# The down projection of a decoder layer as three direct pieces and two Strassen stages, with the sums of activation quarters on GpSimd

## The chip, the cores and the metric

One Trainium2 chip, one core. The kernel is a program of five engines written out by hand: TensorE (PE, matmuls; PEld its weight loads), VectorE (DVE), ScalarE (ACT), GpSimd (POOL) and SyncE (SP), which here only issues DMAs. The metric is the device time of one execution in microseconds (us).

## The reference

One layer of a decoder in float32: a token mixer, a cross attention and a gated channel mixer, each on a normalised input and added to the residual stream, then a last normalisation. The change concerns the last product, `w_down`, of shape 5632 x 2048, on 512 tokens:

```python
D_MODEL, SEQ, D_FF = 2048, 512, 5632

def swiglu(h, w_gate_up, w_down):
    gu = h @ w_gate_up
    g, u = gu[..., :D_FF], gu[..., D_FF:]
    return (jax.nn.silu(g) * u) @ w_down

def reference(x, mem, g_mix, w_in, ...):
    ...
    h = h + swiglu(rms_norm(h, g_ffn[l]), w_gate_up[l], w_down[l])
    return rms_norm(h, g_final)
```

## The kernel before

**Precision.** Every float32 operand is split into a high part `hi` (ACT copies it into the float32r type) and a remainder `lo` (DVE subtracts, `lo = x - hi`). A product is the three matmuls hi*hi, hi*lo and lo*hi, summed in PSUM.

**Direct form** (`columns`, L695 to L709). A weight tile of 128 rows by 512 columns, one *step*, is cut into four column tiles j. For each j three matmuls run over 512 tokens (L702, L703, L704): 12 matmuls a step, into the four PSUM banks of a group. DVE and ACT split the weights one step at a time into a ring of four slots (`w_hi`, `w_lo`; `SPL = 4`), so they can be at most four steps ahead of PE. Weights come in by SP, two steps in a DMA of 512 KB, into `raw`, which holds four such pairs.

**Strassen stage** (`Stage`, `product`, `products`). Where the contraction runs over 16 tiles of 128 and the result has two column tiles ("gate" and "up") and two token halves of 256, a block needs seven products of half size instead of eight: P1, Q5, P2, P6, P7, P4, P3 in this order in PE, interleaved with those of the next block (`cycle_products`). A product is eight *wide* matmuls (L936: hi weights by 512 columns, which are the hi and the lo part of 256 tokens side by side) and eight *narrow* ones (L947: lo weights by 256 columns). P6, P7 and P4 start with the narrow ones. Three of the seven (P1, P2, P4) use quarters of the activations as they are, the other four use sums s1 to s4 of quarters. For each block DVE splits 14 half products of weights (`block_lo`, L1945), forms four sums of weights (`sum_x1` to `sum_x4`, L1953 to L1972) and takes the results out of PSUM (`gate_first`, `gate_joined`, `up_first`, `up_second`, `up_joined`), with ACT's copies of partial sums and `gate_second` beside them. The weight slots are eight. The mixer's gates (`mix`, 16 blocks) and gate and up of the channel mixer (`ffn`, 40 blocks) have this form.

**Down projection.** The 44 tiles of the hidden activation have been spilled to DRAM (`hidden_spilled`, by POOL, one when `hidden_out` has made it) and come back by `hidden_load`; ACT and DVE split them again (`hidden_hi` L1548, `hidden_lo` L2296). It is in the direct form: two halves hh of 22 tiles (`HH = 22`), in each four column groups c, in each 22 steps k, 176 steps in all. DVE adds each finished group to the residual `acc`, which has been reloaded from DRAM (`down_out`, `last_sum` L2447).

**The end.** The last sums, their squares (ACT) and the addition of squares (DVE `add_square`, L2160) lead to one small set of matmuls (`square_sums`), 16 transposes, the scaling and the stores.

**Order.** Every engine runs its list in order and waits on semaphores. SP's queue holds all loads in one order, POOL's queue the spills. A wait in ACT's or DVE's list holds back everything that stands behind it, the splitting of weights for PE above all.

Of the kernel before, what the change touches and what calls it, by code (L numbers as in the profile page):

```python
# [22 lines left out]
F32 = mybir.dt.float32  # L23
# [25 lines left out]
HH = HT // 2  # L49
# [37 lines left out]
G_LAST = G_DOWN + 4  # L87
# [34 lines left out]
class Stage:  # L122
# [5 lines left out]
    last_group: int  # L128
    reg_a: list
# [43 lines left out]
def build(nc, x, mem, g_mix, w_in, conv_w, sinks, w_attn_o, w_conv_o, w_out, g_xattn, g_mem,  # L173
          w_xq, w_xkv, w_xo, g_ffn, w_gate_up, w_down, g_final, rope, out):
    with ExitStack() as ctx:
# [57 lines left out]
        up_t = at("up_t", 120 * KB, [P, 2, 2, SEQ])  # L233
        gfin = at("gfin", 176 * KB, [P, D])
# [65 lines left out]
        PLACES = [s_res[:, i, :, :] for i in range(12)] + [h_both[:, :, k, :] for k in range(0, KT, 2)]  # L300
        PLACES += [h_both[:, :, k, :] for k in range(1, KT, 2)] + [s_res[:, i, :, :] for i in (14, 15)]

        def place(h):

            return h if h < len(PLACES) else h - len(PLACES)
# [27 lines left out]
        def regions(X, Y):  # L333
# [5 lines left out]
        s_x = [sem(f"x_loaded{t}") for t in range(TT)]  # L339
# [79 lines left out]
        mix = Stage(0, KT, 4, mix_snap, G_OPROJ + 7, *regions(A, B), m_both,  # L419
                    *mix_slots, *block_sems)  # L420
        ffn = Stage(KT, BLOCKS, 0, ffn_snap, G_U0, *regions(B, A), s_both,
                    *ffn_slots, *block_sems)
        s_xsum = sem("x_summed")
# [20 lines left out]
        s_hld = [sem(f"hidden_loaded{i}") for i in range(8)]  # L444
# [11 lines left out]
        def _(sp):  # L456
# [118 lines left out]
            def hidden_load(h):  # L575

                n = place(h)
                if h >= len(PLACES):
                    sp.wait_ge(s_used, B_DOWN + 3 * HH + n + 1 - (G_DOWN + 3))
                elif h < 4:  # L580
                    sp.wait_ge(ffn.used, ffn.number("Q5", BLOCKS - 1) + 2)
                elif h < 8:
                    sp.wait_ge(ffn.used, ffn.number("P6", BLOCKS - 1) + 2)
                elif h < 12:
                    sp.wait_ge(ffn.used, ffn.number("P7", BLOCKS - 1) + 2)
                else:
                    sp.wait_ge(ffn.used, ffn.halves())
                sp.wait_ge(s_hsp[h % 2], 16 * (h // 2 + 1))
                if h >= 8:
                    sp.wait_ge(s_hld[h % 8], 16 * (h // 8))  # L590
                sp.dma_start(PLACES[n][:, 1, :].bitcast(F32), hid_dram[h]).then_inc(s_hld[h % 8], 16)

            def down_load(hh, c, p):

                load((B_DOWN + HH * (4 * hh + c)) // 2, 0, None, p, wd, hh * HH * P + 256 * p, 512 * c)

            for p in range(RAW):
                sp.wait_ge(ffn.lo, ffn.number("P7" if p == 1 else "P3" if p == 3 else "P4", BLOCKS - 2) + 2)
                sp.dma_start(raw[:, p, :, :], wd[256 * p:256 * p + 256, 0:512].rearrange("(b p) n -> p b n", p=P)).then_inc(s_raw[p], 16)
            for h in range(12):  # L600
                hidden_load(h)
            for hh in range(2):
                for c in range(4):
                    for p in range(HH // 2):
                        if hh == 0 and c == 0 and 4 <= p < 9:
                            hidden_load(2 * p + 4)
                            hidden_load(2 * p + 5)
                        if hh or c or p >= RAW:
                            down_load(hh, c, p)
                        if hh == 0 and 1 <= c < 3 and p < 4:  # L610
                            hidden_load(HH + 4 * (c - 1) + p)
                        if hh == 0 and p == 9:
                            if c == 0:
                                for i in range(2):
                                    sp.wait_ge(s_hsp[i], 16 * (HT // 2))
                            sp.dma_start(acc[:, 4 * c:4 * c + 4, :], acc_dram[c]).then_inc(s_ald[c], 16)
                        if hh and c == 0 and 2 * p + len(PLACES) < HT:
                            hidden_load(len(PLACES) + 2 * p)
                            hidden_load(len(PLACES) + 2 * p + 1)
# [8 lines left out]
        def _(pool):  # L628
# [55 lines left out]
            pool.wait_ge(ffn.used, ffn.halves())  # L684
# [4 lines left out]
        def _(pe):  # L689
# [185 lines left out]
            def product(st, name, b):  # L875

                first, last = 4 * (st.last_group - 1), 4 * st.last_group
                if name == "P1":
                    r = st.reg_a[b % 2]
                    if b == 0:  # L880
                        pe.wait_ge(s_freed, first + 1)
                        if st is mix:
                            pe.wait_ge(s_ulo, KT)
                    elif b == 1:
                        pe.wait_ge(s_freed, first + 4)
                    else:
                        pe.wait_ge(st.g2, st.base + b - 1)
                elif name == "Q5":
                    r = st.reg_c[b % 2]
                    if b == 0:  # L890
                        pe.wait_ge(s_freed, first + 2)
                        if st is mix:
                            pe.wait_ge(s_mslo, 8)
                        else:
                            pe.wait_ge(s_slo, 16)
# [28 lines left out]
                if st is ffn and b == 0 and name == "P2":  # L924
                    pe.wait_ge(s_pl, KT)
                n, on = st.number(name, b), name in ("P6", "P7", "P4", "P3")
# [158 lines left out]
            for hh in range(2):  # L1085
                for c in range(4):
                    g = G_DOWN + 4 * hh + c
                    b0 = B_DOWN + HH * (4 * hh + c)
# [1410 lines left out]
```

## Time and profile before

| | |
|---|---|
| time, median of 3 runs | 2650.07 us (2649.94 to 2652.64) |
| the profiled execution, first to last instruction | 2649.0 us |
| PE busy | 2625.9 us (99%), 13393 matmuls |
| DVE busy | 1858.1 us (70%) |
| ACT busy | 1222.7 us (46%) |
| POOL busy | 56.0 us (2%) |
| DMA | 343.18 MB, mean 130 GB/s |

The profiled execution's own time is its span, 2649.0 us, 1.1 us below the median of the runs; the profile shows nothing around the span. Shares of busy time are averages over stages with different limits: in the two Strassen stages DVE is busy nearly all the time, in the down projection about a third of it. Matmuls overlap in the pipeline, so the duration of one (0.39 us) is longer than its distance from the next; the pace is read from start to start.

### The profile page before, as it was taken

How to read it: one execution, taken by the hardware profiler on the slowest of the kernel's cores; microseconds unless marked ns; L12 is line 12 of the kernel's file. 1: busy time of each engine (PE TensorE's matmuls, PEld its weight loads, DVE VectorE, ACT ScalarE, POOL GpSimd, SP SyncE). 2: the span in 40 equal slices, each digit the busy share in tenths (PEclk: the TensorE clock that was granted, in tenths of full speed). 3: DMA queues.
4: the chain of work that ended last, by engine and by line, in shares of the span. 5: the costliest groups of instructions: out<-in, count | busy, mean ns of one | idle time of the engine just before them, and what ended most of it. 6: DMA issues, size and time to landing. Idle time of an engine off the chain costs nothing.

```text
span 2649.0 us, 35447 instructions
## 1 busy us (share of the span) xinstructions
PE 2625.9 (99%) x13393; PEld 2243.3 (85%) x13393; DVE 1858.1 (70%) x3163; ACT 1222.7 (46%) x2275; POOL 56.0 (2%) x106
## 2 busy tenths in 40 slices
PE   8999999999999999999999999999999999999998
PEld 7888788888888888888888888888888888888887
DVE  5557876755999964457889999999999973234334
ACT  6335553434555543345655555555555542233221
POOL 0000000000000000000000000000000000000000
PEclk9999999999999999999999999999999999999999
DMA  6332222545445473233444343443434463343222
GB/s 232 95 95 81 72 80 83 194 145 164 143 140 166 132 276 110 96 105 121 149 116 135 116 134 110 122 129 116 133 111 121 131 222 135 124 143 120 96 99 92
DMA packets 331933, 343.18 MB, mean 130 GB/s; under 512 B 11420, under 2 KB 240884, under 8 KB 329204
## 3 DMA queue, kind: packets, MB, share of 16 engines
q1 hardware_dynamic: 320756, 292.68, 35.4%
q0 software_dynamic: 11008, 48.24, 4.7%
q8 instruction: 107, 1.75, 0.3%
q14 instruction: 62, 0.51, 0.1%
HBM read 304.17 MB, written 36.70 MB: 129 GB/s over the span
## 4 chain that ended last, share of the span: by engine, by line
PE 98%; DVE 1%; ACT 0%; issue 0%; DMA 0%; DVEq 0%; ACTq 0%
PE bank L936 27%; PE bank L702 16%; PE bank L703 16%; PE bank L704 16%; PE bank L947 14%; PE bank L717 2%; PE bank L719 2%; PE bank L718 2%; PE bank L823 0%; PE bank L756 0%; DVE y_out L2474 0%; PE bank L1051 0%; PE bank L1023 0%; PE bank L811 0%; PE bank L837 0%
## 5 line engine op out<-in xcount | busy, mean ns | idle before, releaser
L1666 DVE TENSOR_TENSOR w_lo<-raw,w_hi 128x512 fp32r<-128x512 f32 x352 | 243.7, 692 | 478.3 <-ACT w_hi L1130 477.5
L1130 ACT ACTIVATE w_hi<-raw 128x512 fp32r<-128x512 f32 x352 | 222.3, 631 | 584.7 <-PE bank L704 580.1
L702 PE MATMUL bank<-h_both,w_hi 128*128 128x512 f32 x864 | 340.9, 395 | 0.3 <-DVE v_c L1828 0.3
L703 PE MATMUL bank<-h_both,w_hi 128*128 128x512 f32 x864 | 336.9, 390 | 0.0
L704 PE MATMUL bank<-h_both,w_lo 128*128 128x512 f32 x864 | 336.6, 390 | 0.0
L1945 DVE TENSOR_TENSOR w_lo<-braw,w_hi 128x512 fp32r<-128x512 f32 x392 | 251.3, 684 | 9.5 <-ACT w_hi L1308 9.5
L1668 DVE SCALAR_TENSOR_TENSOR w_lo<-raw,par,w_hi 128x512 fp32r<-128x512 f32 x208 | 155.2, 750 | 144.0 <-ACT w_hi L1130 142.9
L1130 ACT ACTIVATE w_hi<-raw,par 128x512 fp32r<-128x512 f32 x208 | 149.3, 721 | 194.9 <-PE bank L704 123.3
L1308 ACT ACTIVATE w_hi<-braw 128x512 fp32r<-128x512 f32 x392 | 222.3, 625 | 34.2 <-PE bank L947 16.1
L704 PEld LDWEIGHTS bank<-h_both,w_lo 128*128 128x128 f32 x864 | 162.2, 188 | 34.9
L702 PEld LDWEIGHTS bank<-h_both,w_hi 128*128 128x128 f32 x864 | 162.3, 188 | 32.5 <-issue 0.5
L703 PEld LDWEIGHTS bank<-h_both,w_hi 128*128 128x128 f32 x864 | 162.4, 188 | 31.1
L1945 DVE TENSOR_TENSOR h_both<-braw,h_both 128x512 fp32r<-128x512 f32 x280 | 179.3, 684 | 0.0
L1308 ACT ACTIVATE h_both<-braw 128x512 fp32r<-128x512 f32 x280 | 158.7, 625 | 14.9 <-PE bank L947 12.4
L702 PE MATMUL bank<-s_res,w_hi 128*128 128x512 f32 x416 | 161.8, 389 | 0.0
L703 PE MATMUL bank<-s_res,w_hi 128*128 128x512 f32 x416 | 161.8, 389 | 0.0
L704 PE MATMUL bank<-s_res,w_lo 128*128 128x512 f32 x416 | 161.8, 389 | 0.0
L936 PE MATMUL bank<-s_both,w_hi 128*128 128x512 f32 x640 | 157.6, 391 | 0.0
L936 PE MATMUL bank<-s_both,h_both 128*128 128x512 f32 x640 | 157.5, 391 | 0.0
L1329 ACT ACTIVATE snap_b<-bank 128x512 f32<-128x512 f32 x54 | 32.3, 599 | 260.6 <-PE bank L936 260.6
L936 PEld LDWEIGHTS bank<-s_both,h_both 128*128 128x128 f32 x640 | 117.6, 188 | 22.7
L936 PEld LDWEIGHTS bank<-s_both,w_hi 128*128 128x128 f32 x640 | 117.6, 188 | 22.7
(289 smaller groups left out, 5343.9 us busy)
## 6 DMA issues: line engine op xcount, KB each, us to landing
braw<-in_w_gate_up_dram SPq DMA_DIRECT2D x160, 512.0 KB, 5.2
raw<-in_w_down_dram SPq DMA_DIRECT2D x88, 512.0 KB, 3.6
raw<-in_w_in_dram SPq DMA_DIRECT2D x80, 512.0 KB, 3.5
braw<-in_w_in_dram SPq DMA_DIRECT2D x64, 512.0 KB, 5.0
raw<-in_w_out_dram SPq DMA_DIRECT2D x32, 512.0 KB, 3.6
hidden_spilled<-up_t POOLq DMA_DIRECT2D x44, 256.0 KB, 5.7
raw<-in_w_attn_o_dram SPq DMA_DIRECT2D x16, 512.0 KB, 3.7
raw<-in_w_conv_o_dram SPq DMA_DIRECT2D x16, 512.0 KB, 3.7
```

What stands on the lines that cost most here:

```text
L702: pe.matmul(o_, w_hi[:, s, c], hi, start=(k == 0), stop=False)
L703: pe.matmul(o_, w_hi[:, s, c], lo, start=False, stop=False)
L704: mm = pe.matmul(o_, w_lo[:, s, c], hi, start=False, stop=(k == n - 1))
L717: pe.matmul(bk[j][:, :], hi[:, c], w_hi[:, s, :], start=(k == 0), stop=False)
L718: pe.matmul(bk[j][:, :], hi[:, c], w_lo[:, s, :], start=False, stop=False)
L936: mm = pe.matmul(r, st.slot_hi[st.slot(n + half)][:, q, :], both, start=(not on and half == 0 and q == 0), stop=(on_last == "wide" and hal ...
L947: mm = pe.matmul(r[:, 1, :], st.slot_lo[st.slot(n + half)][:, q, :], u_h, start=False, stop=(on_last == "narrow" and half == 1 and q == 3) ...
L1130: nc.scalar.activation(w_hi[:, s, :], raw[:, n % RAW, (b0 + k) % 2, :], ACT.Copy, scale=sc).then_inc(s_hi, 1)
L1308: nc.scalar.activation(st.slot_hi[s], weights(name, b)[:, 4 * half:4 * half + 4, :], ACT.Copy).then_inc(st.hi, 1)
L1666: nc.vector.tensor_tensor(w_lo[:, s, :], src, w_hi[:, s, :], ALU.subtract).then_inc(s_lo, 1)
L1668: nc.vector.scalar_tensor_tensor(w_lo[:, s, :], src, g[:, k:k + 1], w_hi[:, s, :], ALU.mult, ALU.subtract).then_inc(s_lo, 1)
L1945: nc.vector.tensor_tensor(st.slot_lo[s], weights(name, b)[:, 4 * half:4 * half + 4, :], st.slot_hi[s], ALU.subtract).then_inc(st.lo, 1)
```

## The change

The 44 tiles are cut as 4 + 16 + 4 + 16 + 4 (`CK = 4`, `SK = 16`). The three pieces of 4 stay in the direct form (16 steps each, 48 in all). The two pieces of 16 become Strassen stages `down[0]` and `down[1]` of `DB = 8` blocks each, on the regions, slots and semaphores of `ffn`. The four quarters of a stage's activation are loaded by four DMAs of 1 MB (`quad_load`); POOL makes the four sums (`quad_sums`); ACT and DVE split the seven forms (`form_hi`, `form_lo`) in between the steps of the direct piece ahead of the stage, the seventh (form 6) in block 0. The results of the first two direct pieces and of the two stages are no longer added by DVE to a resident `acc`: ACT (direct pieces) or the usual block outputs put them into `gate_t` and `up_t`, and POOL adds them to the residual in DRAM by accumulating DMAs (`group_added`, `block_added`), two slots deep (`s_add`). The last direct piece is added by DVE to the residual reloaded as `acc_end`.

```diff
+        down = [Stage(KT + BLOCKS + DB * i, DB, 0, ffn_snap, G_DOWN + 4 * i + 3, B_DOWN + 4 * CK * (i + 1), 4 + 12 * i, *regions(B, A),
+                      ([s_both[3], s_both[1], s_both[2], s_both[0]], s_both)[i], *ffn_slots, *block_sems) for i in range(2)]
+        d_sum4 = tile4[:, :, :].rearrange("p k (a n) -> p (k a) n", a=2)
...
+            def act_load(i):
+                st = (ffn, *down)[i // CK]
+                sp.wait_ge(ffn.used, st.number("Q5", st.blocks - 1) + 2)
...
+                sp.dma_start(act_place(i)[:, 1, :].bitcast(F32), hid_dram[act_tile(i)]).then_inc(s_hld[i % CK], 16)
+            def quad_load(i, n):
+                st = (ffn, *down)[i]
+                h0, e, t2 = (CK + SK) * i + CK, n % 2, n // 2
+                sp.wait_ge(ffn.used, st.number(("P1", "P2", "P6", "P4")[n], st.blocks - 1) + 2)
...
+                src = hid_dram[h0:h0 + SK].rearrange("(k e) p (t n) -> e t p k n", e=2, t=2)[e, t2]
+                sp.dma_start(dst, src).then_inc(s_qld[n], 16)
...
+            for i in range(3):
+                for p in range(RAW):
+                    down_load(i, p)
+                for k in range(CK):
+                    act_load(CK * i + k)
...
+                for n in (0, 2, 1, 3):
+                    quad_load(i, n)
+                for p in range(RAW, 8):
+                    down_load(i, p)
+                    if p == 5:
+                        for q in (1, 0, 2, 3):
+                            down_block_load(i, 1, q)
+                for q in range(4):
+                    down_block_load(i, 0, q)
+                for b in range(2, DB):
+                    for q in (1, 0, 2, 3):
+                        down_block_load(i, b, q)
...
+            def quad_sums(i, step):
+                s1, s2, s3 = d_sums[i]
+                a11, a12, a22 = (quad_forms(i, n)[0] for n in (0, 2, 5))
+                if step == 0:
+                    pool.wait_ge(down[i].used, 14 * down[i].base)
+                    for n in (2, 3, 0, 1):
+                        pool.wait_ge(s_qld[n], 16 * (i + 2))
+                    nc.gpsimd.tensor_tensor(s1, raw_21, a22, ALU.subtract).then_inc(s_dsum, 1)
+                    nc.gpsimd.tensor_tensor(s3, a11, raw_21, ALU.subtract).then_inc(s_dsum, 1)
+                else:
+                    pool.wait_ge(s_dsum, 4 * i + 1)
+                    nc.gpsimd.tensor_tensor(s2, s1, a11, ALU.subtract).then_inc(s_dsum, 1)
...
+                    nc.gpsimd.tensor_tensor(d_sum4, a12, s2, ALU.add).then_inc(s_dsum, 1)
+            def group_added(u, c):
+                pool.wait_ge(s_freed, 4 * (G_DOWN + (u // 12) * 4 + c) + 4)
+                for g, t in enumerate((gate_t, up_t)):
+                    pool.dma_start(acc_dram[c][:, 2 * g:2 * g + 2, :], t[:, u % 2, :, :], accum_op=ALU.add).then_inc(s_add[u % 2], 16)
+            def block_added(st, b):
+                pool.wait_ge(st.gf, st.base + b + 1)
+                pool.dma_start(acc_dram[b // 2][:, 2 * (b % 2), :], gate_t[:, b % 2, 0, :], accum_op=ALU.add).then_inc(s_add[b % 2], 16)
...
+            for i in range(2):
+                quad_sums(i, 0)
+                quad_sums(i, 1)
+                for c in range(4):
+                    group_added(12 * i + c, c)
+                for b in range(DB):
+                    block_added(down[i], b)
...
-            for hh in range(2):
+            for i in range(3):
                 for c in range(4):
...
+                    for k in range(CK):
+                        wait_block(B_DOWN + CK * (4 * i + c), 0, None, k)
...
+                        columns(banks(g), k, CK, act[:, 0, :], act[:, 1, :], wait_bank=free)
+                if i < 2:
+                    products(down[i])
...
+            def form_hi(i, n):
+                if n in (0, 2, 5):
+                    act.wait_ge(s_qld[{0: 0, 2: 1, 5: 3}[n]], 16 * (i + 2))
+                else:
+                    act.wait_ge(s_dsum, 4 * i + {1: 1, 4: 2, 3: 3, 6: 4}[n])
...
+                nc.scalar.activation(hi_, src, ACT.Copy).then_inc(s_dhi, 1)
+            def group_out(i, c, j):
+                g, u = G_DOWN + 4 * i + c, 12 * i + c
+                if u < 2:
+                    act.wait_ge(s_hsp[u], 16 * (HT // 2))
+                else:
+                    act.wait_ge(s_add[u % 2], 32 * (u // 2))
+                act.wait_ge(s_done, 4 * g + j + 1)
+                nc.scalar.activation(evicted(c, j), banks(g)[j][:, :], ACT.Copy).then_inc(s_freed, 1)
+            FORMS = {7: 0, 8: 2, 9: 5, 11: 1, 12: 4, 13: 3}
+            def classic_part(i, n):
+                hi(B_DOWN + CK * (4 * i + n // CK), G_DOWN + 4 * i + n // CK, n % CK)
+                if i < 2 and n in FORMS:
+                    form_hi(i, FORMS[n])
+                if i < 2 and n % CK == CK - 1 and n >= 2 * CK - 1:
+                    for j in range(4):
+                        group_out(i, n // CK - 1, j)
...
@@ gate_second (ACT), gate_first and up_second (DVE)
+                elif st in down:
+                    dve.wait_ge(s_add[b % 2], 32 * ((st.unit + b) // 2))
...
+            def form_lo(i, n):
+                dve.wait_ge(s_dhi, 7 * i + {0: 1, 2: 2, 5: 3, 1: 4, 4: 5, 3: 6, 6: 7}[n])
+                src, hi_, lo_ = quad_forms(i, n)
+                dve.wait_ge(s_dsum, 4 * i + {0: 3, 2: 4, 5: 1}.get(n, 4))
+                nc.vector.tensor_tensor(lo_, src, hi_, ALU.subtract).then_inc(s_dlo, 1)
+            FORMS = {10: 0, 11: 2, 12: 5, 13: 1, 14: 4, 15: 3}
+            def classic_part(i, n):
+                lo(B_DOWN + CK * (4 * i + n // CK), 0, None, n % CK)
+                if i < 2 and n in FORMS:
+                    form_lo(i, FORMS[n])
...
-            for c in range(1, 4):
-                for k in range(HH):
-                    lo(B_DOWN + HH * (4 + c), 0, None, k)
-                    if 3 <= k < 7:
-                        last_sum(4 * c - 7 + k)
-                    if 7 <= k < 11:
-                        last_square(4 * c - 11 + k)
+            for n in range(SPL, 4 * CK):
+                classic_part(2, n)
+                if n >= 2 * CK:
+                    last_sum(n - 2 * CK)
+                if n >= 2 * CK + 2:
+                    last_square(n - 2 * CK - 2)
+            for t in range(8, 12):
+                last_sum(t)
+                last_square(t - 2)
```

## Rows read from the trace of the kernel before

**Rows 1.** The page: busy time and share by engine, then tenths per 40th.

```profile
PE 2625.9 (99%) x13393; PEld 2243.3 (85%) x13393; DVE 1858.1 (70%) x3163; ACT 1222.7 (46%) x2275; POOL 56.0 (2%) x106
...
DVE  5557876755999964457889999999999973234334
...
PEclk9999999999999999999999999999999999999999
```

**Rows 2.** Waits of PE in the whole span: total us, times, longest.

```profile
PE bank L756 <- DMA x_nat<-in_x_dram: 6.0, 1, 6.0
...
PE bank L733 <- DVE ssq L2160: 3.5, 1, 3.5
```

**Rows 3.** The chain that ended last, pieces of `ffn`: start, us, what.

```profile
1404.06 3.65 PE bank L936 x16
...
1715.95 3.65 PE bank L936 x16
...
2142.89 1.91 PE bank L947 x16
2144.81 3.65 PE bank L936 x16
2148.46 0.95 PE bank L947 x8
2149.41 0.23 PE bank L702
```

**Rows 4.** PE, last matmul of the down projection, from the timeline.

```profile
2627.77 0.39 PE L704 MATMUL bank<-h_both,w_lo 128*128 128x512 f32 x1
```

**Rows 5.** Busy time by stretch (a block; first 16 direct steps; the rest): PE, PEld, DVE, ACT, POOL, clock, DMA share, GB/s.

```profile
1900.00:1919.50 19.50, 19.50 (x114) 17.23 (x113) 18.05 (x27) 10.32 (x20) 0.55 (x1) 1.00 0.41 121
...
2149.50:2193.00 43.50, 43.50 (x193) 36.03 (x192) 24.03 (x38) 17.88 (x32) 1.08 (x2) 1.00 0.66 236
...
2197.00:2633.00 436.00, 432.50 (x1910) 358.14 (x1908) 150.88 (x228) 120.22 (x196) 0.00 (x0) 1.00 0.32 109
```

**Rows 6.** Groups by line, DVE and ACT, 1400 to 2120 us; last row whole span.

```profile
L1945 DVE TENSOR_TENSOR w_lo<-braw,w_hi 128x512 fp32r<-128x512 f32 x260 | 166.4, 684 | 0.0
...
L1960 DVE TENSOR_TENSOR braw<-braw 128x1024 f32<-128x1024 f32 x37 | 45.3, 1226 | 3.9
...
L2332 DVE TENSOR_TENSOR gate_t<-gate_t,rbc 128x512 f32<-128x512 f32 x37 | 25.6, 692 | 1.3
...
L1308 ACT ACTIVATE h_both<-braw 128x512 fp32r<-128x512 f32 x260 | 147.4, 625 | 12.0 <-PE bank L947 11.8 <-DMA braw<-in_w_gate_up_dram 0.2
...
L1185 ACT ACTIVATE x_sq<-x_nat 128x2048 f32<-128x2048 f32 x4 | 7.6, 1901 | 0.0
```

**Rows 7.** Groups of POOL, whole span: its only work on tiles.

```profile
L639 POOL TENSOR_SCALAR_AFFINE_SELECT mask<-mask 128x256 f32<-128x256 f32 x1 | 0.4, 401 | 0.1
...
L633 POOL TENSOR_SCALAR_AFFINE_SELECT ident<-ident 128x128 f32<-128x128 f32 x1 | 0.3, 285 | 0.1
```

**Rows 8.** DMA issues, whole span: count, KB each, median us to landing.

```profile
hidden_spilled<-up_t POOLq DMA_DIRECT2D x44, 256.0 KB, 5.7
...
branches_spilled<-tile POOLq DMA_DIRECT2D x7, 1024.0 KB, 6.7
...
residual_spilled<-acc POOLq DMA_DIRECT2D x4, 1024.0 KB, 4.8
acc<-residual_spilled SPq DMA_DIRECT2D x4, 1024.0 KB, 6.5
...
mrg_t<-merged_spilled SPq DMA_DIRECT2D x3, 1024.0 KB, 8.1
```

**Rows 9.** Timelines around the start of the down projection: POOL, then DVE.

```profile
2154.92 0.54 POOL L683 DMA_DIRECT2D hidden_spilled<-up_t  x1 [10.55 <-DVE up_t L2345]
...
2166.46 0.69 DVE L1666 TENSOR_TENSOR w_lo<-raw,w_hi 128x512 fp32r<-128x512 f32 x1 [1.37 <-ACT w_hi L1130]
...
2169.24 0.69 DVE L1666 TENSOR_TENSOR w_lo<-raw,w_hi 128x512 fp32r<-128x512 f32 x1 [1.49 <-ACT w_hi L1130]
```

More of the change, by code:

```diff
@@ L298, in merged_place, with act_place, act_tile, evicted @@
             return mrg_t[:, (k + KP) % KT, :, :]
[L300 to L305, printed above, removed]
+        def act_place(i):
+            return s_res[:, (0, 12, 0)[i // CK] + i % CK, :, :]
+        def act_tile(i):
+            return (CK + SK) * (i // CK) + i % CK
+        def evicted(n, j):
+            return (gate_t, up_t)[j // 2][:, n % 2, j % 2, :]
         hid_dram = nc.dram_tensor("hidden_spilled", [HT, P, SEQ], F32, kind="Internal").ap()
@@ L593, in down_load @@
[L593 to L601, printed above, removed]
-            for hh in range(2):
[L603 to L619, printed above, removed]
@@ new lines, in down_load @@
+            def down_load(i, p):
+                row, col = (CK + SK) * i * P + 256 * (p % 2), 512 * (p // 2)
+                src = wd[row:row + 256, col:col + 512].rearrange("(b p) n -> p b n", p=P)
+                n = (B_DOWN + 4 * CK * i) // 2 + p
+                if p < RAW:
+                    st = (ffn, *down)[i]
+                    sp.wait_ge(ffn.lo, st.number("P7" if p == 1 else "P3" if p == 3 else "P4", st.blocks - 2) + 2)
+                else:
+                    sp.wait_ge(s_lo, 2 * (n - RAW) + 2)
+                sp.dma_start(raw[:, n % RAW, :, :], src).then_inc(s_raw[n % RAW], 16)
@@ new lines, in down_block_load @@
+            def down_block_load(i, b, q):
+                st, before = down[i], (ffn, *down)[i]
+                if b == 0:
+                    sp.wait_ge(s_lo, B_DOWN + 4 * CK * i + 8 + 2 * q + 2)
+                else:
+                    last, n = (before, before.blocks - 1) if b == 1 else (st, b - 2)
+                    sp.wait_ge(ffn.lo, last.number(("P7", "P4", "P3")[0 if q == 1 else 2 if q == 3 else 1], n) + 2)
+                row, col = ((CK + SK) * i + CK) * P, 2 * P * b + P * (q % 2)
+                src = wd[row:row + SK * P].rearrange("(k e p) n -> e p k n", e=2, p=P)
+                sp.dma_start(braw[b % 2][:, q, :, :], src[q // 2][:, :, col:col + P]).then_inc(ffn.raw[b % 2][q], 16)
@@ L2428, in _ @@
[L2428 to L2441 removed]
+            for n in range(SPL, 4 * CK):
+                classic_part(0, n)
```

275 lines of the change are left out of this document (189 added, 86 removed).

## The prediction

> **What bounds the kernel now.** The page comes first: PE is busy 99% of the span, and the granted clock is at its full level in all 40 slices [rows 1]. The waits of PE say whether anything stands before it: of the whole span only 6.0 us at the start and 3.5 us at the end (the last sum of squares) are long, and none lies where the down projection begins or runs [rows 2]. So the time is PE's list of matmuls, and the change is worth what it takes off that list, less the stalls that it brings. The pace is read from the chain that ended last: 16 wide matmuls of a Strassen stage take 3.65 us, 8 narrow ones 0.95 us, and a direct one stands 0.23 us from the next [rows 3]. The stretches then show the cover. DVE is busy 18.05 of 19.5 us in a block of `ffn`, so nearly the whole time, and 24.0 of 43.5 us in the first 16 direct steps; in the rest of the down projection about a third [rows 5].
>
> **What PE no longer does.** From 1404.06 to 1715.95 us the chain shows the same place of 16 blocks: 311.9 us, so 19.49 us a block and 2.785 us a product [rows 3]. The down projection starts at T = 2149.4 [rows 3] and its last matmul at 2627.8 [rows 4]: 176 steps in 478.6 us, 2.72 us a step, without a gap. Two stages of 8 blocks are 16 x 19.49 = 311.9 us. They replace 32 of the 44 tiles, 128 steps x 2.72 = 348.2 us. The other 48 steps cost what they did, and the end behind them holds the same instructions (the 3.5 us wait with them). The gain is **36.3 us** ahead of stalls. It is a tenth of 348 and not an eighth, as a narrow matmul takes 0.119 us and not half of a wide one's 0.228 [rows 3].
>
> **What a direct piece now must cover.** From here times count from T, the end of the Strassen stage before it; the piece lasts 16 x 2.72 = 43.5 us. The quarter that comes last is asked for when P4 of the last block is done, at -2.8. A load of 1 MB lands in 6.5 to 8.1 us [rows 8], so at +4 to +5. For the first piece POOL has one spill ahead in its list, issued at 2154.9 = +5.5 [rows 9]; for the second it has the adds of block 7, ready about as late. The sums begin at about +6. In the same stretch of before the DMA engines are busy 0.66 of the time [rows 5]; the loads come in the order of need and I put no stall on them.
>
> *A sum on POOL* (2048 elements a partition, two inputs) isn't in the trace. POOL's passes over 128 and 256 elements took 285 and 401 ns [rows 7]: by the slope 2048 elements take 2.0 us, with one input. Eight of the longer ones at two inputs are 8 x 0.40 x 2 = 6.4 us. I take the middle, 4.2 us, as two inputs at the slope are 3.9. Four in a row end at +22.8 (14 to 32 at the ends). In a sentence of its own: the Trainium skill (GPSIMD Engine Reference, "Performance versus the Vector engine") gives 4497 ns for such an addition, by which they would end at +24.
>
> *ACT.* A form of 2048 elements takes 1.90 us, a split of 512 takes 0.63 [rows 6]. It may split step n when step n-4 has left PE, at 2.72(n-3). With forms at n = 7, 8, 9, 11, 12, 13 and four evictions of 0.6 us behind n = 7, 11, 15 it is through with n = 8 at +16.4, n = 10 at +21.4, n = 12 at +27.3, n = 15 at +33.2.
>
> *DVE.* A form of 2048 elements: 0.68 us for 512 and 1.22 for 1024 [rows 6] give 2.3. Its list is lo(10), form 0, lo(11), form 2 and so on. lo(10) ends at +22.1, form 0 at +24.4, form 2 (which needs the fourth sum) at +27.4, lo(12) at +28.1; PE wants lo(12) at 12 x 2.72 = +32.6. lo(15) ends at +37.0 (wanted at +40.8), the last form at +39.3, and P1's lo at +40.7 (wanted at +45.3). In before lo(9) starts at 2166.5 = +17.1, 7.4 us ahead of its step [rows 9]; the forms use up about half of that lead. Stall: 0. Block 0 then holds form 6 (2.3 us) more than a later block. A later block costs DVE 14 x 0.68 + 4 x 1.22 + 5 x 0.69 = 17.9 of 19.5 us [rows 6], less than in `ffn`, where gate and up are also scaled and multiplied. With form 6, block 0 is at 20.2 us and draws on the slots; I price it from 0 to 1.3 us a stage.
>
> *Port.* DVE's splits read two tiles in SBUF, and POOL's sums do so too; no row has both at once. Free of each other, the cost is 0. If each waits for the other's whole instruction, they alternate: sums of 4.2 us from +6.7 let through lo(6), lo(7), lo(8) and end at +25.3, lo(9) is ready at +25.9 where +24.5 is wanted: a stall of 1.4 us, and what follows fits. The trace has no row that decides it. The Trainium skill (SBUF — State Buffer, "Who interferes with whom") speaks against the change here: the port pair shared by the two is an exclusive lock, and a DVE instruction with two SBUF inputs contends with a GpSimd instruction that reads SBUF; by it the stall would be this 1.4 us and not 0, and no row here shows which.
>
> *Accumulating DMAs.* 1 MB for a group, 0.5 MB for a block, behind the sums in POOL's list. Plain spills of 1 MB land in 4.8 and 6.7 us, a load in 6.5 [rows 8]. An accumulation reads and writes the target: from 6.7 (all hidden in each other) to 6.5 + 6.7 = 13.2 us (one after the other). Call it X. The first goes out at +23.8, groups follow in line. ACT's second eviction of group 3 and its split for P2 stand behind group 1's add, wanted at about +47: 23.8 + 2X. DVE's `gate_first` of block 0 stands behind group 2's add, and with it the splits for the next Q5, wanted by +60.5: 23.8 + 3X. Both bear X up to about 12 us. At 13.2 the second is late by 2.9 us a stage, at 6.7 nothing is.
>
> **The sum.** 2650.1 - 36.3 = 2613.8 us. On top for two stages: 0 to 2.8 for the port, 0 to 2.6 for block 0, 0 to 5.8 for the adds; I take 3 us in all, one stall of about 1.5 us a stage. **2617 us**, with 2613.5 to 2622 as the range of this case. The median is 1.1 us above the profiled span, and the difference is taken to stay.
>
> **The rivals.**
>
> *The sums are slow and hold DVE off.* At 6.4 us each and whole instructions in turn, lo(7) is 1.7 us late, lo(8) another 4.2, lo(9) another 4.3: 10.2 us a stage, and forms 0 and 2 come so late that no lead is left. Two stages: 2613.8 + 20.4 = 2634. For it: the splits are on the path of every step, and nobody else can do them. Against it: at 4.2 us the same mechanism costs next to nothing; and without the lock even sums of 6.4 us (end +31.6, form 2 +33.9, lo(12) +34.5) cost 2 us.
>
> *The accumulating DMAs are slow; slower than before.* The queue of three groups comes out late, ACT and DVE stand in their lists at `group_out` and `gate_first`, and the weight splits behind them stop PE. Each us of X beyond 12 costs 3 us a stage. From X = 12.2 + 18.2/3 = 18 us the gain of 36.3 is gone; at 20 us it would be 2613.8 + 2 x 23.3 = 2660. For it: three groups in 33 us on top of the weights. Against it: 20 us for 1 MB is half as long again as a load and a spill of 1 MB in series [rows 8]. In a sentence of its own: the Trainium skill (Collectives: The Full Stack, "Why ReduceScatter is half of AllGather") says that an addition in the DMA is slower only by its second read, thus half the rate; on the 6.7 us row that would be at most 13.4 us and on the safe side of 18, and no row here shows it.
>
> *The blocks do not run at 19.49 us.* A loss of 36.3 / 16 = 2.3 us in every block would bring the time back to 2650, no change. It would need DVE or DMA to be the limit in a steady block. DVE has 1.6 us of room, DMA runs at 0.41 [rows 5] and gets 0.5 MB of accumulation on top. A little for it, hardly all of it.
>
> **How the numbers follow.** Forecast (2617, small stalls) 0.60. Slow sums or an equally long stall at the stage starts (2624 to 2638) 0.21. Partial loss in the blocks (2638 to 2645) 0.05. No change 0.04. Slow accumulations 0.07. Better than 2613, as PE's pace in direct steps or at the end may gain in a way that I don't see, 0.03. The range **2612 to 2637** holds the first two cases. A measurement of this kernel tells about 0.2% (5.3 us) from no change. Faster by more than that: 0.60 + 0.21 + 0.03 + 0.05 = 0.89; within 0.04; slower 0.07.
>
> **What would show it.** PE's list: 1536 direct matmuls of 512 columns fewer (of 2112), 896 wide and 896 narrow more; the span from `ffn`'s end to the end of the last direct step 478.6 - 36.3 = 442.3 us plus stalls. The waits of PE name the stalls: on `w_lo` of a direct step in the second half of a piece it is the sums or the forms; on the hi or lo slots in block 0 after a wait of ACT or DVE on `residual_spilled`, the adds; on P1 to P7 of all blocks, the third rival. A POOL sum near 4 us, and DVE splits no longer than 0.69 us beside it, would bear out the port's price of 0; splits of several us would show the lock. X is the time from issue to landing of the DMAs from `gate_t` and `up_t`. The prediction is wrong if the quarters land much later than +5, if X is over 12 us, or if the sums take over 5 us with the lock.

## The result and the profile after

| | before | after |
|---|---|---|
| time, median of 4 runs | 2651.36 us (2649.94 to 2652.64) | 2632.73 us (2630.60 to 2634.75) |
| ratio, 95% interval | | 0.9931 [0.9917, 0.9946] |
| profiled execution, first to last instruction | 2649.0 us | 2629.8 us |
| forecast | | 2617 us, range 2612 to 2637 |

The kernel is 18.6 us faster (17.3 against the 2650.07 us that the prediction started from); the list of PE alone said 36.3. The page of after stands against [rows 1]: DVE is busier at the end, POOL is busy for 135.9 us instead of 56.0, PE is still at 99%.

```profile
PE 2596.3 (99%) x13649; PEld 2232.3 (85%) x13649; DVE 2064.9 (79%) x3369; ACT 1321.6 (50%) x2449; POOL 135.9 (5%) x162
...
DVE  5557876654999974456879999999999998879886
...
POOL 0000000000000000000000000000000022013100
```

The waits of PE (us in total, times, longest) against [rows 2]: the first and the last two rows are new, and these lie in the down projection.

```profile
PE bank L805 <- DVE w_lo L1842: 5.9, 4, 2.0
...
PE bank L836 <- DVE ssq L2340: 3.5, 1, 3.5
...
PE bank L1056 <- DVE w_lo L2121: 2.6, 2, 1.3
PE bank L1056 <- DVE h_both L2121: 1.7, 2, 1.1
```

The three new groups are 10.2 us. The stretches (PE, PEld, DVE, ACT, POOL, clock, DMA share, GB/s) show what else there is, against [rows 5]: a granted clock below full in the five microseconds around the end of PE's first wait (0.67, so partly at the lower level of 1.2 GHz), and a DVE without a gap.

```profile
2164.40:2169.40 5.00, 4.46 (x19) 3.07 (x17) 5.00 (x2) 5.00 (x6) 5.00 (x2) 1.00 0.11 40
2169.40:2174.40 5.00, 3.55 (x9) 2.79 (x10) 5.00 (x2) 0.61 (x2) 4.92 (x2) 0.67 0.32 106
...
2193.00:2353.00 160.00, 158.07 (x901) 139.04 (x900) 132.88 (x186) 82.40 (x151) 13.60 (x16) 1.00 0.65 149
```

**The ledger.** PE's timeline gives the start of each direct piece and each stage (first L805 on `s_res`, first L1045). A clean piece is 43.5 us, a clean stage 155.9 us. Between executions the start of the down projection varies by 3 us and what follows its last matmul by 1 us, so all kernels below are compared by these four lengths, in us. Each row is one execution; of the experiments, e1, e4, e5 and e7 were timed four times, the others once.

| kernel | piece 1 | stage 1 | piece 2 | stage 2 | over the clean sum |
|---|---|---|---|---|---|
| after | 48.3 | 158.5 | 49.3 | 159.3 | 16.6 |
| e1 sums in quarters | 47.5 | 162.9 | 48.0 | 161.2 | 20.8 |
| e2 memsets for the sums | 43.5 | 156.8 | 43.6 | 158.0 | 3.1 |
| e3 plain stores | 52.7 | 155.9 | 48.0 | 155.9 | 13.7 |
| e4 sums on DVE | 43.6 | 157.6 | 43.5 | 157.4 | 3.3 |
| e5 quarters, forms in another order | 50.1 | 158.6 | 50.2 | 158.3 | 18.4 |
| e6 as e4, plain stores | 43.6 | 155.9 | 43.6 | 155.9 | 0.2 |
| e7 as e4, third add later | 43.6 | 155.9 | 43.6 | 155.9 | 0.2 |
| e8 copies for the sums | 43.6 | 157.2 | 43.6 | 157.5 | 3.1 |
| e9 after, third add later | 50.0 | 155.9 | 46.8 | 155.9 | 9.8 |
| e10 two more sums | 53.3 | 161.9 | 55.8 | 160.1 | 32.3 |

So 10.6 of after's 16.6 us are lost in the pieces and 6.0 in the stages, where the ordinary blocks run at 19.49 us and only block 0 is late.

**In the pieces.** POOL's timeline and DVE's, of the first piece:

```profile
2155.58 4.61 POOL L755 TENSOR_TENSOR s_f<-raw,h_both 128x2048 f32<-128x2048 f32 x1
2160.14 5.10 POOL L756 TENSOR_TENSOR s_f<-h_both,raw 128x2048 f32<-128x2048 f32 x1
2165.19 5.05 POOL L759 TENSOR_TENSOR s_f<-s_f,h_both 128x2048 f32<-128x2048 f32 x1
2170.32 4.88 POOL L763 TENSOR_TENSOR tile<-h_both,s_f 128x2048 f32<-128x2048 f32 x1
```

```profile
2154.54 0.69 DVE L1842 TENSOR_TENSOR w_lo<-raw,w_hi 128x512 fp32r<-128x512 f32 x1
2155.70 21.26 DVE L1842 TENSOR_TENSOR w_lo<-raw,w_hi 128x512 fp32r<-128x512 f32 x6 [0.48 <-ACT w_hi L1239]
```

Six splits, which took 0.69 us each in [rows 9], fill 21.26 us. The durations of these six by form (minimum, median, maximum in ns):

```profile
L1842 DVE TENSOR_TENSOR w_lo<-raw,w_hi x6: 677/5046/5111, 2155.7 to 2176.3; 128x512 fp32r<-128x512 f32 x6
```

Four of them, lo(5) to lo(8), last as long as a sum (lo(n) is the split for step n). PE's timeline shows the consequence, a wait for lo(7) and then matmuls at double distance (0.43 instead of 0.23 us):

```profile
2170.85 0.58 PE L805 MATMUL bank<-s_res,w_hi 128*128 128x512 f32 x1 [1.99 <-DVE w_lo L1842]
2171.23 0.63 PE L806 MATMUL bank<-s_res,w_hi 128*128 128x512 f32 x1
2171.66 0.63 PE L807 MATMUL bank<-s_res,w_lo 128*128 128x512 f32 x1
2172.09 0.63 PE L805 MATMUL bank<-s_res,w_hi 128*128 128x512 f32 x1
...
2175.81 0.50 PE L805 MATMUL bank<-s_res,w_hi 128*128 128x512 f32 x1 [0.35 <-DVE w_lo L1842]
```

From its first matmul at 2149.37, 2.72 us a step, PE should begin step 7 at 2168.4 and step 8 at 2171.1. It begins them at 2170.85 and 2175.81, so 2.4 and 4.7 us late. lo(8) ends only at 2175.76: the slow matmuls merely fill time in which PE would have waited for it. In the second piece the order is another. The sums start 8.3 us into it and hold lo(6) to lo(9); the last late split starts step 9 at 2384.71, 4.0 us late, and the clock falls after that:

```profile
2364.46 4.61 POOL L755 TENSOR_TENSOR s_f<-raw,h_both 128x2048 f32<-128x2048 f32 x1 [4.10 <-issue]
```

```profile
2384.71 0.50 PE L805 MATMUL bank<-s_res,w_hi 128*128 128x512 f32 x1 [1.97 <-DVE w_lo L1842]
```

```profile
2384.70:2389.70 5.00, 4.99 (x15) 3.94 (x16) 5.00 (x4) 1.24 (x3) 2.84 (x4) 0.66 0.85 117
```

No later split makes PE wait there, so the eight matmuls at 0.43 us make the piece 1.7 us longer.

**In block 0.** The chain runs through the fourth weight load (start, us), and DVE's timeline has the wait for it:

```profile
2191.01 11.52 DMA braw<-in_w_down_dram
```

```profile
2202.55 1.23 DVE L2136 TENSOR_TENSOR braw<-braw 128x1024 f32<-128x1024 f32 x1 [3.29 <-DMA braw<-in_w_down_dram]
```

11.5 us to landing; the median of all loads of this kind is 6.0. In the second stage DVE's wait is 4.1 us. What follows tells the two causes apart.

### The profile page after: what moved, and what is told of

It is laid out like the page before. It is cut to its first block, busy times and chain, and to the rows that moved or that the text cites. A ratio compares the mean times of both kernels' runs of the same rounds, so it can differ in the third digit from the quotient of the medians.

```text
span 2629.8 us, 36723 instructions
## 1 busy us (share of the span) xinstructions
PE 2596.3 (99%) x13649; PEld 2232.3 (85%) x13649; DVE 2064.9 (79%) x3369; ACT 1321.6 (50%) x2449; POOL 135.9 (5%) x162
## 4 chain that ended last, share of the span: by engine, by line
PE 93%; DVE 4%; DMA 1%; issue 1%; ACT 1%; DVEq 0%; ACTq 0%
PE bank L1045 34%; PE bank L1056 18%; PE bank L805 11%; PE bank L806 11%; PE bank L807 11%; PE bank L820 2%; PE bank L822 2%; PE bank L821 2%; DVE w_lo L1842 2%; DMA braw<-in_w_down_dram 1%; DVE s_both L2591 1%; PE bank L926 0%; DVE y_out L2700 0%; DVE h_both L2591 0%; PE bank L859 0%
## 5 line engine op out<-in xcount | busy, mean ns | idle before, releaser
L2121 DVE TENSOR_TENSOR w_lo<-braw,w_hi 128x512 fp32r<-128x512 f32 x504 | 322.6, 683 | 14.7 <-ACT w_hi L1419 14.7
L1419 ACT ACTIVATE w_hi<-braw 128x512 fp32r<-128x512 f32 x504 | 285.3, 625 | 52.6 <-PE bank L1056 19.4
L1239 ACT ACTIVATE w_hi<-raw 128x512 fp32r<-128x512 f32 x224 | 141.4, 631 | 297.9 <-PE bank L807 293.1
L2121 DVE TENSOR_TENSOR h_both<-braw,h_both 128x512 fp32r<-128x512 f32 x392 | 250.9, 683 | 2.7 <-ACT h_both L1419 2.5
L1419 ACT ACTIVATE h_both<-braw 128x512 fp32r<-128x512 f32 x392 | 222.0, 625 | 28.3 <-PE bank L1056 17.3
L805 PE MATMUL bank<-h_both,w_hi 128*128 128x512 f32 x576 | 228.8, 397 | 0.3 <-DVE v_c L2004 0.3
L807 PE MATMUL bank<-h_both,w_lo 128*128 128x512 f32 x576 | 224.6, 390 | 0.0
L1045 PE MATMUL bank<-s_both,w_hi 128*128 128x512 f32 x896 | 220.6, 391 | 0.0
L1045 PE MATMUL bank<-s_both,h_both 128*128 128x512 f32 x896 | 220.5, 391 | 0.0
L1045 PEld LDWEIGHTS bank<-s_both,h_both 128*128 128x128 f32 x896 | 164.7, 188 | 31.8
L1045 PEld LDWEIGHTS bank<-s_both,w_hi 128*128 128x128 f32 x896 | 164.5, 188 | 31.7
L1045 PE MATMUL bank<-h_both 128*128 128x512 f32 x672 | 167.5, 391 | 0.0
L1045 PE MATMUL bank<-h_both,w_hi 128*128 128x512 f32 x672 | 167.4, 391 | 0.0
L1045 PEld LDWEIGHTS bank<-h_both,w_hi 128*128 128x128 f32 x672 | 122.8, 188 | 23.3
L1045 PEld LDWEIGHTS bank<-h_both 128*128 128x128 f32 x672 | 122.6, 188 | 23.1
L1056 PE MATMUL bank<-s_both,w_lo 128*128 128x256 f32 x896 | 125.6, 283 | 2.6 <-DVE w_lo L2121 2.6
```

What stands on the lines that cost most here:

```text
L805: pe.matmul(o_, w_hi[:, s, c], hi, start=(k == 0), stop=False)
L807: mm = pe.matmul(o_, w_lo[:, s, c], hi, start=False, stop=(k == n - 1))
L1045: mm = pe.matmul(r, st.slot_hi[st.slot(n + half)][:, q, :], both, start=(not on and half == 0 and q == 0), stop=(on_last == "wide" and hal ...
L1056: mm = pe.matmul(r[:, 1, :], st.slot_lo[st.slot(n + half)][:, q, :], u_h, start=False, stop=(on_last == "narrow" and half == 1 and q == 3) ...
L1239: nc.scalar.activation(w_hi[:, s, :], raw[:, n % RAW, (b0 + k) % 2, :], ACT.Copy, scale=sc).then_inc(s_hi, 1)
L1419: nc.scalar.activation(st.slot_hi[s], weights(name, b)[:, 4 * half:4 * half + 4, :], ACT.Copy).then_inc(st.hi, 1)
```

## The experiments

Theory A: a sum on POOL holds a split on DVE off for its whole length. Rivals: B, the sums merely end late; C, the DMA queues are full and the weights late; D to G as the expectations name them.

**e1, sums in quarters.**

```diff
+            def pool_sum(out, x, y, op):
+
+                n = KP // 4
+                for c in range(4):
+                    ks = slice(n * c, n * c + n)
+                    last = nc.gpsimd.tensor_tensor(out[:, ks, :], x[:, ks, :], y[:, ks, :], op)
+                last.then_inc(s_dsum, 1)
...
-                    nc.gpsimd.tensor_tensor(s1, raw_21, a22, ALU.subtract).then_inc(s_dsum, 1)
+                    pool_sum(s1, raw_21, a22, ALU.subtract)
...
```

> Each of POOL's four sums is cut into four instructions of 512 elements a partition; the same sums, the same order. Theory A (each sum of the changed kernel, 4.6 to 5.1 us, holds DVE off for its whole length, so that a weight split of 0.68 us takes as long as the sum): a split can now be held for 1.3 us at most, the six splits beside the sums fit into their 2.72 us steps, the waits of PE in the direct pieces (5.9 us) go, both pieces end within 1 us of 43.5 us instead of 48.2 and 49.1, and lo(15) is early enough that block 0 loses less too: 2622 to 2625 us. Rival B (the sums end too late, +25.6 instead of +22.8, and the forms wait for them): four instructions have three more starts, the sums end later and the time stays at 2632 or rises to 2635. Rival C (the loads in the full DMA queues are what is late): no change, 2632.

Measured: 2634.40 us (2633.44 to 2635.05), ratio to before 0.9935 [0.9919, 0.9952]. Theory A's number is missed. The timeline of DVE, then of POOL, says why:

```profile
2167.76 1.75 DVE L1850 TENSOR_TENSOR w_lo<-raw,w_hi 128x512 fp32r<-128x512 f32 x1 [1.21 <-ACT w_hi L1247]
2170.08 1.13 DVE L1850 TENSOR_TENSOR w_lo<-raw,w_hi 128x512 fp32r<-128x512 f32 x1 [0.57 <-ACT w_hi L1247]
2173.73 3.42 DVE L2599 TENSOR_TENSOR h_both<-h_both 128x2048 fp32r<-128x2048 f32 x1 [2.51 <-POOL s_f L752]
...
2181.36 2.29 DVE L2599 TENSOR_TENSOR h_both<-h_both 128x2048 fp32r<-128x2048 f32 x1 [2.51 <-POOL tile L752]
```

```profile
2155.74 6.06 POOL L752 TENSOR_TENSOR s_f<-raw,h_both 128x512 f32<-128x512 f32 x4
...
2173.70 7.55 POOL L752 TENSOR_TENSOR tile<-h_both,s_f 128x512 f32<-128x512 f32 x4
```

No split takes 5 us any more; beside the sums they take 0.7 to 1.8 us: the hold is per instruction, as A says. But a sum in four parts takes 6.0 to 7.6 us instead of 4.9, the last ends at 2181.2 instead of 2175.2, and DVE, which comes to forms 0 and 2 at steps 10 and 11, waits 2.5 us for each in its list. The larger part of e1's loss is in block 0, 7.0 and 5.3 us. DVE waits 5.4 and 5.0 us for the fourth load there: in the first stage this load takes 12.4 us and, as lo(15) is late too, goes out 4.3 us ahead of the stage and not 6.7 as in after. A is right on the hold and wrong on what it would bring.

**e2, writes only.** The sums become memsets of the same tiles.

```diff
-nc.gpsimd.tensor_tensor(s1, raw_21, a22, ALU.subtract).then_inc(s_dsum, 1)
+nc.gpsimd.memset(s1, 0.0).then_inc(s_dsum, 1)
...
```

> POOL's four sums are left out: it clears the four tiles with a memset instead, which writes 2048 elements a partition and reads nothing, so the down projection's result is not the reference's. Theory A (the reading of POOL holds the splits off): the splits beside the memsets stay at 0.69 us, both direct pieces take 43.5 us, 2618 to 2624 us with what block 0 still loses. If writing held DVE off as well, the splits beside the memsets would take about 2 us, and the pieces about 44.5 us. Rival C (full DMA queues): 2632.

Measured: 2619.05 us; both pieces clean, the splits beside the memsets (1.8 us each) undisturbed:

```profile
2157.38 1.83 POOL L755 MEMSET s_f<- 128x2048 f32 x1
2159.12 1.83 POOL L756 MEMSET s_f<- 128x2048 f32 x1
```

```profile
2157.51 0.69 DVE L1842 TENSOR_TENSOR w_lo<-raw,w_hi 128x512 fp32r<-128x512 f32 x1 [0.47 <-ACT w_hi L1239]
2160.29 0.69 DVE L1842 TENSOR_TENSOR w_lo<-raw,w_hi 128x512 fp32r<-128x512 f32 x1 [2.08 <-ACT w_hi L1239]
```

The pieces' loss is the sums' doing, and POOL's writing is not what holds DVE. Rival C is out for the pieces; 3.1 us remain in the stages, where DVE waits 1.6 and 2.8 us for the fourth load.

**e3, plain stores.**

```diff
-pool.dma_start(acc_dram[c][:, 2 * g:2 * g + 2, :], t[:, u % 2, :, :], accum_op=ALU.add)
+pool.dma_start(acc_dram[c][:, 2 * g:2 * g + 2, :], t[:, u % 2, :, :])
...
```

> The adding DMAs become plain stores to the same places: the additions to the residual are left out, and with them the second read of each DMA, so the result is not the reference's. Theory A (POOL's sums hold the splits off): the direct pieces stay at 48.2 and 49.1 us and the time falls by at most 2 us in block 0, 2630 to 2632. Rival C (the adds fill the DMA queues and make weights late, in the piece and in block 0): the waits of DVE on block 0's last weight load (3.3 and 4.1 us) and most of PE's waits go, 2618 to 2624.

Measured: 2629.48 us. The stages come out clean (155.9 both), so that much of C is right and there alone. The first piece is the worst but e10's, 52.7 us, and one split shows why (by form, ns; then PE's wait for it):

```profile
L1842 DVE TENSOR_TENSOR w_lo<-raw,w_hi x1: 14059/14059/14059, 2157.3 to 2157.3; 128x512 fp32r<-128x512 f32 x1
```

```profile
2171.39 0.80 PE L805 MATMUL bank<-s_res,w_hi 128*128 128x512 f32 x1 [6.66 <-DVE w_lo L1842]
```

This split was held by three sums in a row and not by one. That plain stores made this so isn't shown; the start of POOL's first sum stood 0.1 us ahead of the split's here and in after alike.

**e4, sums on DVE**, one each behind steps 7 to 10.

```diff
-                quad_sums(i, 0)
-                quad_sums(i, 1)
...
+                if i < 2 and 7 <= n < 11:
+                    quad_sum(i, n - 7)
```

> The four sums move from POOL to DVE, one each behind steps 7, 8, 9 and 10 of the direct piece, 2.3 us each by the splits of the same size. Theory A (POOL's 19.6 us of sums block DVE almost fully for that long; DVE itself needs 9.1 us for them): DVE gains about 10 us in each piece, the pieces take 43.5 to 45 us, 2619 to 2625 us. Rival B (sums that end late are what hurts, whoever makes them): with the last one at about +23 instead of +25.6 the forms start 2 us earlier, 2629 to 2632. Rival D (DVE has no room for 9 us more): pieces of over 48 us, 2632 or more.

Measured: 2619.91 us (2618.94 to 2620.97), ratio to before 0.9883 [0.9867, 0.9900]. The sums take 2.28 us each on DVE, the pieces are clean. B and D are out. 3.3 us remain, in block 0, with DVE's wait on the fourth load (1.8 and 1.9 us).

**e5, quarters, and no form ahead of its sum.**

```diff
...
-            FORMS = {10: 0, 11: 2, 12: 5, 13: 1, 14: 4, 15: 3}
+            FORMS = {10: 5, 11: 4, 12: 0, 13: 1, 14: 2, 15: 3}
```

Not shown here: e1's edit, the same change of order on ACT, and the waits that go with it.

> POOL's sums in quarters as in e1, and the forms split in another order (DVE: 5, 4, 0, 1, 2, 3 behind steps 10 to 15, ACT's copies to match), so that DVE comes to no form before its sum is there: with sums that end at +12, +18, +24 and +32 in e1, form 0 moves from step 10 to 12 and form 2 from step 11 to 14. Theory A1 (two costs in one place: a whole sum holds a split for 5 us, and sums cut up hold it for about 1 us but end so late that DVE waits in its list for forms 0 and 2, 2.5 us each): both are gone, the direct pieces take 43.5 to 45 us, 2619 to 2625 us. Rival E (DVE's lost time beside cut sums is what counts, not the order of its list): the pieces stay at 47.5 and 48.0 us, 2630 to 2634.

Measured: 2633.10 us (2632.81 to 2634.45), ratio 0.9935 [0.9918, 0.9952]: missed again, and by a third list. DVE no longer waits for a sum, but its work now lies beside the sums to their end and stretches them; the last ends at 2184.8. POOL issues the first group's add only then, and ACT stands at the eviction of the third group:

```profile
2174.87 9.91 POOL L752 TENSOR_TENSOR tile<-h_both,s_f 128x512 f32<-128x512 f32 x4
```

```profile
2195.89 1.08 ACT L1691 ACTIVATE gate_t<-bank 128x512 f32<-128x512 f32 x2 [13.87 <-DMA residual_spilled<-up_t]
```

PE then waits 4.6 and 4.4 us for the first weights of the stage, and up to there the first piece is only 1.7 us late. So the new order did most of what A1 expected of it in the steps, and the piece lost elsewhere; rival E's range holds the time, but not the pieces' 50 us. This is the mechanism of the second rival of the prediction, reached by late adds and not by slow ones.

**e6, as e4 with plain stores; e7, as e4 with the third add later.** e6 is e3's edit made to e4. e7 adds these lines to e4:

```diff
+                if c == 2:
+                    pool.wait_ge(ffn.raw[0][3], 16 * (down[u // 12].base // 2 + 1))
```

> The sums on DVE as in e4, and plain stores in place of the adding DMAs; the additions to the residual are left out, so the result is not the reference's. What is left in e4 over a clean list of PE is 1.7 and 1.5 us in block 0 of each stage. Theory F (the adds fill the DMA queues at the end of a direct piece, so that block 0's fourth weight load lands in 9 to 11 us and DVE waits 1.8 us for it): DVE's wait on that load goes, both stages take 155.9 to 156.2 us, about 2616.5. Rival G (block 0 is late because DVE carries form 6 and 9 us of sums): stages stay at 157.5 us.

> The sums on DVE as in e4, and POOL issues the add of the third group of a direct piece (and what stands behind it) only when block 0's fourth weight load has landed. Theory F: that load lands 2 to 4 us sooner, DVE's wait on it goes, the stages take 156 to 156.5 us, 2617 to 2618.5 us. Against it: the add now goes out about 9 us later, and gate_first of block 0 stands behind it at about +60; if it lands after that, DVE waits there and nothing is won, 2620 or more.

Measured: e6 2614.01 us, e7 **2614.84 us** (2613.78 to 2616.49), ratio to before 0.9863 [0.9847, 0.9879]. Both are 2 to 3 us below their expectations. In both, DVE has no wait on the fourth load, and every piece and stage is clean. In the first stage that load lands in 5.0 us in e6 and 4.4 in e7, where it took 8.9 in e4. In e7 POOL waits for it and sends the add 43.5 us after the piece began, instead of 35.7 in e4; DVE's second sum of weights comes without a wait:

```profile
2194.18 0.84 POOL L753 DMA_DIRECT2D residual_spilled<-gate_t  x1 [15.02 <-DMA braw<-in_w_down_dram]
```

```profile
2196.38 1.23 DVE L2118 TENSOR_TENSOR braw<-braw 128x1024 f32<-128x1024 f32 x1
```

F is borne out and G is out: it is the adds' traffic at the end of the piece that makes that load late. e7 computes all that after does and beats both kernels.

**e8, one-input copies** in place of the sums.

```diff
-nc.gpsimd.tensor_tensor(s1, raw_21, a22, ALU.subtract).then_inc(s_dsum, 1)
+nc.gpsimd.tensor_copy(s1, raw_21).then_inc(s_dsum, 1)
...
```

> Each of POOL's four sums becomes a copy of one tile of the same size, one input read instead of two; the sums are left out, so the result is not the reference's. Beside memsets (e2) a split took 0.69 us. If POOL's reading of SBUF holds the splits off, whatever the number of inputs, a split beside a copy takes about as long as the copy (2 to 3 us), the copies last 8 to 12 us in all, PE keeps most of its lead, and the pieces take 43.5 to 44.5 us; 2618 to 2622. If only two-input instructions of POOL do it, the splits stay at 0.69 us.

Measured: 2617.97 us. The split beside the second copy took 2.05 us and the next 1.69 us:

```profile
2158.08 1.90 POOL L756 COPY s_f<-h_both 128x2048 f32<-128x2048 f32 x1
2159.92 2.35 POOL L759 COPY s_f<-s_f 128x2048 f32<-128x2048 f32 x1
```

```profile
2158.47 2.05 DVE L1842 TENSOR_TENSOR w_lo<-raw,w_hi 128x512 fp32r<-128x512 f32 x1 [2.09 <-ACT w_hi L1239]
2161.13 1.69 DVE L1842 TENSOR_TENSOR w_lo<-raw,w_hi 128x512 fp32r<-128x512 f32 x1 [0.61 <-ACT w_hi L1239]
```

The memsets of e2 wrote the same tiles and held nothing, so it is POOL's reading of SBUF that holds the split, with one input as with two. At 2 us it stays inside the lead, and the pieces are clean.

**e9, the changed kernel with the third add later; e10, with two more sums.**

The edit of e9 is that of e7, made to the changed kernel.

> The changed kernel with POOL's four sums as they are, and only the add of the third group issued when block 0's fourth weight load has landed (the one edit that took e4 to e7). If the two causes are separate (sums hold the splits in the piece, adds delay that load in block 0), the pieces stay 4 to 6 us over 43.5 us (with e3's 9 us as the worst) and both stages come to 156 to 156.5 us instead of 158.5 and 159.3: 2626 to 2629 us. If the block's loss comes from the piece before it (DVE arrives late), the stages stay over 158 us: 2631 or more.

> The changed kernel with two more instructions of the same size and form on POOL ahead of the four in each stage, into tiles that are overwritten later; the result is unchanged. If each reading instruction of 4.6 to 5.1 us lets DVE through for one split, where PE uses one in 2.72 us, a piece grows by 2 x (5.0 - 2.7) = 4.6 us for them, and by what the lost lead and the lower clock add, and the forms come 10 us later, which DVE waits for: pieces of 55 to 62 us, stages of 157 to 160 us, 2655 to 2665 us. If what counted were the bytes of DMA or the order in which things are queued, 10 us more on POOL would cost at most the waits for the later sums, pieces of under 53 us, below 2645 us.

```diff
+pool.wait_ge(ffn.u1, down[i].base)
+pool.wait_ge(ffn.u2, down[i].base)
+nc.gpsimd.tensor_tensor(d_sum4, a11, a22, ALU.add)
+nc.gpsimd.tensor_tensor(s2, a11, a22, ALU.add)
 nc.gpsimd.tensor_tensor(s1, raw_21, a22, ALU.subtract).then_inc(s_dsum, 1)
```

Measured: e9 2622.94 us, below what was expected; both stages clean, the pieces 6.5 and 3.3 us over. The two causes are separate: the edit takes 6.0 us out of the stages. The two profiled executions are 8.7 us apart; of the rest, 0.8 us lie in the pieces, 1.0 ahead of the down projection and 0.9 behind its last matmul. The pieces differ from after's by when the clock fell, and the second also by the start of the sums. In the first, PE is as late at step 8 as in after (4.7 us), but the clock falls only behind that step and adds 1.7 us. In the second, the sums start 1 us sooner, step 9 is 3.1 us late instead of 4.0, and the clock stays full.

e10 2646.58 us, below its expectation too: pieces of 53.3 and 55.8 us, 5.0 and 6.5 more than after, and stages of 161.9 and 160.1 us. In the first piece the last held split is lo(10) in place of lo(8), and PE is 9.3 us late there and not 4.7: 4.6 us for two sums, as expected. In the second piece the sixth sum also holds form 0 (6.67 us instead of 2.28), and PE waits 4.2 us for lo(11) behind it. The first piece is shorter than the 55 us expected and the second lies in the range; the stages are longer than their 157 to 160. The rival's bounds, pieces under 53 us and a time below 2645, are both passed.

## Why the prediction came out as it did

**The gain of 36.3 us: right.** From the first direct matmul to the last small set (L733, L816, L818) before takes 482.4 us (2149.25 to 2631.66) and e7 takes 446.8 us (2150.65 to 2597.43): 35.6 us less. Direct steps and blocks run at the pace of [rows 3]; most of the 0.7 us that are missing are lost in the last piece. After stays short of this by the 16.6 us of the ledger: 36.3 - 0.7 - 16.6 = 19.0, and the two profiled executions are 19.2 us apart. The ideal time of 2613.8 us is what e6 and e7 measure within 1.1 us.

**"The sum on POOL": mis-sized.** 4.2 us stood as the middle of 2.0 and 6.4; it is 4.6 to 5.1 us beside DVE, and the last of four ends at +25.8 in the first piece and +27.9 in the second, not at +22.8. The Trainium skill (GPSIMD Engine Reference, "Performance versus the Vector engine") gives 4497 ns for such a sum, which is nearer than the 4.2; the trace is 0.1 to 0.6 us above it, beside DVE's splits.

**"The port": the step that failed.** Both ends were named, 0 and 1.4 us a stage, and 3 us taken in all; 4.8 and 5.8 us came. The mechanism of the higher end is the right one. The sizes in it were off. The sums take 4.9 us, not 4.2. In the first piece they start 0.1 us ahead of lo(5) and so hold lo(5) to lo(8), where the working let lo(5) pass and held lo(6) to lo(9) (it started the sums at +6.7, though the loads had given about +6; they started at +6.2): at some 5.05 us each these end at +11.4, +16.4, +21.4 and +26.4, and PE is 2.4 us late at step 7 and 4.7 at step 8. In the second piece they start at +8.3 and not at +6.7, as the last quarter lands only then, and PE is 4.0 us late at step 9. There the lower clock comes on top, 1.7 us, which the sum didn't have at all; in the first piece it costs nothing. The first rival (sums of 6.4 us, 10.2 us a stage, 2634) is the case that happened, with shorter sums and a second cause on top; the chance of 0.21 for it was too low beside 0.60, as nothing in the trace spoke for free passage. That its 2634 is within 1.3 us of the measured time is partly luck: it had 20.4 us in the pieces, where 10.6 were lost, and none of the 6.0 us in the stages. The Trainium skill (SBUF — State Buffer, "Who interferes with whom") calls the port pair an exclusive lock and has a DVE instruction with two SBUF inputs contend with GpSimd's reads and not with its writes; the trace agrees, with 5.05 us for a split beside a sum, 2.05 beside a copy and 0.69 beside a memset.

**"I put no stall on the loads": wrong.** It rested on the DMA share of 0.66 in [rows 5]. The last quarter took 8.4 us in the first piece and 10.6 in the second, where 6.5 to 8.1 were taken, and landed at +5.8 and +8.0 and not at +4 to +5; a landing much later than +5 was one of the prediction's own signs of being wrong. At the end of the first piece the engines are at 0.93 to 1.09 between 2179 and 2199 us (a transfer counts in the stretch in which it starts, so a share can pass 1), and block 0's fourth load, which can't be issued before lo(15) frees its place, takes 11.5 us. Block 0 was priced at 0 to 1.3 us a stage for DVE's form 6; it cost 2.6 and 3.4, and e9, which only delays the third group's add and what stands behind it, gives all of it to the adds. Form 6 itself, which e6, e7 and e9 still carry in block 0, costs nothing.

**The accumulating DMAs.** Adds of 512 KB land in 7.6 us (from `gate_t`) and 10.9 us (from `up_t`, behind it), plain stores in e3 in 3.0 and 5.5. So X is about 11.5 us, between 6.7 and 13.2 as bounded and just below the 12 from which lists would wait (by the prediction's own +47 for ACT, 23.8 + 2X, the bound is 11.6); in the second piece, where two groups were issued within 1.2 us, the later one took 16.0 us. The second rival's mechanism didn't show in after; e5 shows it real. That the adds' traffic would hurt a load was not in the prediction.

**The blocks run at 19.49 us: right**, [rows 3] hold for all blocks but the first; the third rival fell. The 17.9 us of DVE a block were durations added up. The profile has it busy for 16.3 us of a block, since one instruction starts before the one ahead of it has ended (eight splits of 0.683 us fill 5.1 us):

```profile
2255.00:2274.49 19.49, 19.49 (x113) 17.22 (x113) 16.33 (x24) 9.67 (x18) 1.70 (x2) 1.00 0.64 136
```

## What to carry to other kernels

A sum given to POOL is no relief while DVE runs two-input instructions from SBUF that PE waits for (no DVE instruction with fewer inputs stood beside a sum in these runs). Four sums cost POOL 19.6 us and held DVE about as long, and on DVE itself they cost 9.1 us and nothing on PE. In e1 and e5 cutting that work into quarters only shifted the wait to the next list in order (DVE's forms, then ACT's evictions): follow each list once the first wait is gone. Before a transfer is put into a busy end of a stage, look which load is bound to be issued last there, and let the transfer with slack wait for it.

## What the runs showed of the hardware that was not expected

- A held instruction is not always let through after one POOL instruction: in e3 one split of 0.69 us took 14.06 us, three sums long, and PE waited 6.7 us.
- A POOL instruction of 512 elements with two inputs took 1.5 us on average in e1's first sum, and 3.3 us where DVE split a form of 2048 elements beside it (9.91 us for four in e5), so the hold goes both ways.
- After a wait of PE of about 2 us the granted clock fell to the lower level for a while (0.66 and 0.67 over 5 us), with eight or nine matmuls at 0.43 us, but not always: after's first piece has it behind the first wait (1.99 us), its second piece behind the second (1.97), e9's first piece behind the second (1.98) and not the first (1.97), and e9's second piece not at all (0.64 and 1.98). What decides this isn't known.
- What such a fall costs depends on what comes next: nothing in after's first piece, where the next split was later still, and 1.7 us in its second piece and in e9's first.
